# Moving four steps of the context pass to earlier rounds of the last expert sums

## The reference, cut to what matters

```python
u = jnp.take(u_tab, eb, axis=0)
act = jax.nn.gelu(jnp.einsum('tkd,td->tk', u, hb), approximate=False)
vv = jnp.take(v_tab, eb, axis=0)
return jnp.einsum('tk,tkd->td', gb * act, vv)
```

```python
kvc = hc @ w_in[i][:, kv_lo:kv_hi]
...
xc = xc_mid + cg2 * rmsnorm(swiglu(hfc, w_gate[i], w_up[i], w_down[i]), norm_post_ffn[i])
```

## Time and profile before

| | us |
|---|---|
| median of 3 runs | 2854.45 (2853.81 to 2855.3) |
| the profiled execution's own time | 2863.04 |
| its span | 2861.2 |
| TensorE busy | 1903.4 (67%) |
| VectorE busy | 1798.9 (63%) |
| GpSimd busy | 1074.2 (38%) |
| ScalarE busy | 380.1 (13%) |

### The profile page before, as it was taken

How to read it: one execution, slowest core, us unless ns; L and a number is a source line. 1 busy time by engine, 2 the same in 40 slices (tenths; PEclk the granted TensorE clock), 3 DMA queues, 4 the chain that set the end, 5 groups by cost and what they waited for, 6 DMA issues and landing times.

```text
span 2861.2 us, 23645 instructions
## 1 busy us (share of the span) xinstructions
PE 1903.4 (67%) x8197; PEld 1335.0 (47%) x8197; DVE 1798.9 (63%) x3288; ACT 380.1 (13%) x850; POOL 1074.2 (38%) x1047
## 2 busy tenths in 40 slices
PE   7988443176553363454445537878368999988999
PEld 4677111165341151143243126653157787577873
DVE  1437998988767879988888987676774200242001
ACT  1311001122102110002111010000014100041000
POOL 1003444677345655755566755465430000000000
PEclk9999555596675675867668759999579999999999
DMA  8467999999999999999999989999960554324543
GB/s 291 151 209 272 398 398 401 371 380 357 371 388 400 379 400 402 353 348 401 398 404 381 349 324 391 385 399 407 386 227 29 190 156 153 119 75 162 155 154 118
DMA packets 359990, 860.86 MB, mean 301 GB/s; under 512 B 23736, under 2 KB 146880, under 8 KB 359744
## 3 DMA queue, kind: packets, MB, share of 16 engines
q0 software_dynamic: 148288, 538.12, 48.8%
q1 hardware_dynamic: 211584, 321.24, 32.3%
HBM read 858.23 MB, written 1.05 MB: 300 GB/s over the span
## 4 chain that ended last, share of the span: by engine, by line
PE 36%; DMA 22%; DVE 18%; issue 14%; POOL 4%; another core or an unknown queue 3%; ACT 3%; SPq 1%; DVEq 0%; ACTq 0%; POOLq 0%
PE bank L977 14%; DMA RING<-in_peer_v,EX 9%; PE bank L416 6%; PE bank L989 5%; DMA RING<-in_peer_u,EX 4%; POOL RING L1107 2%; DVE ACC L1767 2%; DMA W<-in_w_up 2%; DMA W<-in_w_gate 2%; PE bank L425 2%; PE bank L814 2%; DVE ACC L1785 2%; POOL WORK L1107 1%; PE bank L404 1%
## 5 line engine op out<-in xcount | busy, mean ns | idle before, releaser
L977 PE MATMUL bank<-HT,W 128*128 128x256 f32 x2112 | 485.3, 392 | 67.1 <-issue 28.2
L977 PEld LDWEIGHTS bank<-HT,W 128*128 128x128 f32 x2112 | 414.2, 197 | 137.8 <-issue 40.3
L1107 POOL DMA_INDIRECT RING<-in_peer_v,EX x341 | 382.2, 1121 | 215.0 <-DVE hrows L1785 87.6
L1107 POOL DMA_INDIRECT RING<-in_peer_u,EX x343 | 327.4, 954 | 354.8 <-DVE ACC L1767 198.3
L1767 DVE SCALAR_TENSOR_TENSOR ACC<-RING,hrows 128x1024 bf16<-128x1024 f32 x343 | 403.8, 1218 | 51.2 <-DMA RING<-in_peer_u,EX 29.9
L453 PE MATMUL bank<-W,CACT 128*32 128x512 f32 x696 | 146.5, 940 | 248.3 <-DMA W<-in_w_ada 143.2
L2426 DVE TENSOR_TENSOR WORK<-WORK,bank 128x256 f32<-128x256 f32 x66 | 27.5, 421 | 348.0 <-ACT WORK L1495 343.4
L1107 POOL DMA_INDIRECT WORK<-in_peer_v,EX x171 | 192.8, 1127 | 100.5 <-DVE hrows L1785 40.6
L989 PE MATMUL bank<-W,WORK 128*128 128x512 f32 x528 | 227.3, 592 | 3.6 <-DVE WORK L2426 3.6
L1107 POOL DMA_INDIRECT WORK<-in_peer_u,EX x169 | 160.5, 950 | 183.0 <-DVE ACC L1767 144.3
L1785 DVE SCALAR_TENSOR_TENSOR hrows<-RING,ACTS,hrows 128x1024 f32<-128x1024 f32 x154 | 198.3, 1288 | 38.9 <-DMA RING<-in_peer_v,EX 33.0
(11 more groups left out here) (373 smaller groups left out, 2404.6 us busy)
## 6 DMA issues: line engine op xcount, KB each, us to landing
W<-in_w_ada SPq DMA_DIRECT2D x48, 1024.0 KB
W<-in_ada_w SPq DMA_DIRECT2D x39, 1024.0 KB
W<-in_w_gate SPq DMA_DIRECT2D x33, 1024.0 KB
W<-in_w_up SPq DMA_DIRECT2D x33, 1024.0 KB
W<-in_w_down SPq DMA_DIRECT2D x33, 1024.0 KB
W<-in_w_in SPq DMA_DIRECT2D x32, 1024.0 KB
W<-in_peer_wq SPq DMA_DIRECT2D x22, 1024.0 KB
W<-in_w_out SPq DMA_DIRECT2D x12, 1024.0 KB
```

Source lines behind the costliest of these rows:

```text
L977: mm = pe.matmul(bs[j][:, g * S:(g + 1) * S], w[:, k, j * P:(j + 1) * P], HT[:, k, :], start=(k == 0 and g == 0), stop=(k == DC - 1 and g ...
L1107: gp.indirect_dma_start(SLOT[g % NS], None, rows, bass.IndirectOffsetOnAxis(EX[:, t, k:k + 1], 0))\
```

## The change

One line of VectorE's plan changes. The steps, their instructions and the programs of the other engines stay as they are.

```diff
-            stage(1, 1, 1, {2: [c0], 5: [c0], 21: [c0], 23: [c1], 27: [c1], 30: [first_rows()]})
+            stage(1, 1, 1, {2: [c0], 5: [c0], 15: [c0], 20: [c1], 25: [c1], 27: [first_rows()]})
```

## The result

| | before | after |
|---|---|---|
| median, 20 runs each, us | 2855.74 | 2861.53 |
| lowest to highest | 2851.28 to 2861.57 | 2856.64 to 2869.36 |
| span of the profiled execution | 2861.2 | 2863.5 |
| TensorE, VectorE, GpSimd busy | 1903.4, 1798.9, 1074.2 | 1903.3, 1799.6, 1076.1 |

The ratio is 1.0020, with a 95% interval of 1.0012 to 1.0028: 5.8 us slower (3.4 to 8.0). The forecast was 3.7 us slower. The size sits on the bound of 5.7 us that the prediction drew for a change that can be told; that it is slower at all is clear.

A forecast was written before the change was run, and what follows sets the result against it. Everything after tile 1's last matmul hangs on its end. Last pick 2112.4 plus 11.2, 0.1, 3.85 and 13.5 gave 2141.0 against 2137.3: +3.7 us, so 2858.1; range 2851.5 to 2862.5, the forecast's own 2855 to 2860.

The forecast's parts named there:

- The place that decides: Second context norm, round 23 to 20: VectorE waits some 13 us for ScalarE's root, queued behind copies needing the weights.
- D: Zero point of times: end of the last copy of the context's down projection on ScalarE, 1994.31 before, 1993.50 after.
- The residual's cost of 0: Residual, round 21 to 15: its 8.5 us on VectorE are covered by nine gathers in flight (18.2 us); cost 0.
- Keys and rows: Keys in round 25, rows of tile 0 in round 27: claimed to cause no wait on VectorE.
- GpSimd as the bound of E: After the norm's wait, GpSimd's 34 intervals of 1.51 us set the last pick: 2112.4, +1.3 us.
- E: End of pick 128, the last pick of the last sums on VectorE; 2111.06 before, forecast 2112.4.
- The way from the last gather's issue to E: End of the last sums: some 3.5 us from last issue (2107.6) to landing (2111.1), last pick ended at 2112.4.
- TensorE's clock: Latent tile 1: clock at 0.50 after idling, transposes and lowering +1.1, matmuls +2.9, less 1.69 us: +2.3 us.
- M: End of tile 1's 48 matmuls on TensorE, on which all later work hangs; forecast 2141.0 against 2137.3, +3.7 us.
- the slower rival: Last sums: GpSimd held more often, 1.59 us an interval; +6.5 to +8.5 us, 2862; chance 0.20.
- The rival without a stall: Norm in round 20: no wait or a short one, as weights come sooner; -2 us, 2852; chance 0.12.
- that of 1.24 us an interval: Last sums: GpSimd issues at 1.24 us an interval, DMA and VectorE bound; +1 us, 2855.5; chance 0.13.

The follow-up runs named there:

- root_between: Changed kernel with ScalarE's root of the second context norm moved up behind the fifth of eight modulation copies; ratio to before 1.0005, to the changed kernel 0.9982.
- res15_norm20: Kernel before with the residual moved from round 21 to 15 and the norm from 23 to 20, keys and rows as before (27, 30); ratio to before 1.0011.
- res15: Kernel before with only the residual moved, from round 21 to 15; profiled and timed twice, ratios to before 1.0001 and 1.0009.
- no_root: Changed kernel with the second context norm's square root left out, so VectorE waits for no ScalarE there (computes less); ratio to before 0.9986.
- root_between30: Changed kernel with ScalarE's root moved up behind the fifth modulation copy and tile 0's rows back in round 30; ratio to before 1.0003.
- rows29: Kernel before with the residual in round 15 (was 21) and tile 0's rows in 29 (was 30), norm and keys as before; ratio to before 0.9998.
- norm17: Changed kernel with the second context norm in round 17 in place of 20; ratio to before 1.0031.

## Why the prediction was right

**The place that decides** was named: predicted VectorE idle "some 13 us" at the second context norm, ended by ScalarE's root behind the last column copy; measured 12.90 us. Predicted free ScalarE at D + 58.6, measured 57.5, and 58.7 and 58.8 in the two repetitions. The landing of one chunk in 7.35 us held (chunks 5 to 8 came 7.25 to 7.6 us apart in these three profiles).

**The residual's cost of 0** held: it ran at 1993.72 to 2002.2 behind a wait of 1.65 us, and pick 84 started at D + 38.4 (38.9 before). Keys and rows waited for nothing, as predicted.

**GpSimd as the bound of E** held in its rate: 34 intervals from 2054.32 to 2105.34, 1.50 us each against 1.51. The Trainium skill (SBUF — State Buffer, section "Who interferes with whom") infers that a DVE instruction with two SBUF inputs doesn't hold up the generation of descriptors. By that an interval here would be 0.94 + 0.30 = 1.24 us, and the trace doesn't agree: issues of 1.98 and 1.99 us stood again beside such instructions (2058.84, 2063.61, 2068.38). What held them isn't shown: in `root_between`, where VectorE waited some 0.4 us before many of its picks, the mean was 1.64.

**Two sizes were off and in part cancelled.** The way from the last gather's issue to E was put at 4.8 us (3.5 to landing without a queue, and one pick). It was 7.7: the DMA moved data until about 5.3 us after the issue, and then VectorE was still one pick behind. So E was D + 119.5 and not D + 118.1. TensorE's clock was put at +2.3 us, with tile 0's 13.53 us as the nearest row; tile 1's matmuls took 12.61 after, 12.72 and 12.75 in the repetitions, and transposes and lowering 3.72 and not 3.85, so it was +1.3 to +1.5. M came at D + 147.1, predicted 146.7: +4.1 and +3.7 us. That these two are so close is in part luck: E was 1.4 us worse than predicted, the clock 1.0 us better. The timed 5.8 us is above both; with an interval from 3.4 to 8.0 it doesn't contradict them. The median of 2861.53 itself lies above the forecast's own 2855 to 2860 and near the slower rival's 2862; 1.3 us of that is the kernel before, whose median went from 2854.45 to 2855.74 with more runs.

**The split**, from single profiles counted from D: the norm's place costs 5.3 to 6.0 us in E (`res15_norm20` against the two of `res15`; 0.4 to 2.7 from pick 64), the queue ahead of its root 3.6 to 6.0 with the rows in 27 (`root_between`, `no_root`) and 1.6 with the rows in 30; the rows' place 1.4 to 1.6 in the way from E to M; the residual's own move is between 0 and -3. The timed runs back the first two together (`root_between` and `res15` against the changed kernel), not each size.

**The slower rival** (GpSimd held at 1.59 an interval) didn't occur in the changed kernel, whose rate was 1.50, 1.52 and 1.45 in its three profiles. Its rate did in the three kernels that have the norm in 20 without the wait: 1.61 in `no_root`, 1.64 in `root_between`, 1.59 in `root_between30`. So with VectorE's plan the same (`root_between`) the rate came out otherwise, for a reason that isn't shown; that the rate of before carried over to the changed kernel was in part luck. The rival without a stall fell to the row of 12.90 us, that of 1.24 us an interval to the 1.50.

## What to carry to other kernels

Before a step is moved to an earlier place on one engine, read what stands ahead of its partner's instruction on the other engine's queue, and when that comes: here a root of 0.2 us stood behind copies that waited for 8 MB of weights. Here the cheaper cure was to move the partner up into a gap of its own, as in `root_between`, though that only brought the time of before back. And an engine that is freed early may be paid for in its clock: here work that ran through to the next part made the way from E to M 1.4 us and more shorter than work that was done sooner and left a gap.

## What was not expected of the hardware

- The granted clock of TensorE fell from 1.00 to 0.50 around a gap of 3.03 us (rows29), where the earlier trace rows had shown it for some 6 us. The price was 3.0 us on 48 matmuls (13.61 against 10.60).
- A pause of the gathers isn't lost to the weights: in `norm17` TensorE had the chunks behind the norm 7.6, 5.2 and 3.7 us after one another and the last two together, against 7.4 us apart beside full gathers. A wait half as long again moved the last pick, from D, by 1.2 us at most.
